# Five and four seven-product pairs in a feed-forward pass, raw low parts on GpSimd

## The chip, the core and the metric

One core of a Trainium2 chip runs the whole kernel. The metric is device time in microseconds from one launch, median of three runs. Its engines run side by side, each with its own instruction queue, and are kept in order by semaphores: TensorE multiplies, VectorE and ScalarE and GpSimd do elementwise work, SyncE issues the loads. TensorE, VectorE and ScalarE read and write the accumulator banks, and all of them share the on-chip memory SBUF.

## What is computed

One layer of a hybrid decoder on 256 tokens with a model width of 2048: a latent attention and a state-space branch, merged and projected, then a SwiGLU feed-forward part, then a gated per-layer embedding. The change lies in the feed-forward part:

```
f = rms_norm(h, ffn_norm_pre)                       # 256 x 2048
f = (silu(f @ w_gate) * (f @ w_up)) @ w_down        # w_gate, w_up: 2048 x 5632
h = h + rms_norm(f, ffn_norm_post)
```

All is float32, and the result has to be close to float32.

## The kernel before

**Precision.** A float32 value is held as a high part (`whi`, rounded to TensorE's fp32r) and a low part (`wlo = raw - whi`, fp32r too). One product of a 128x128 block of tokens with 512 weight columns is three matmuls: high by high, high by low, low by high (`one_tile`; matmuls L851 to L853).

**Passes and chunks.** The feed-forward phase `ff` has 11 passes (0 to 10). A pass covers 512 columns of `w_gate` and the same 512 of `w_up`, side by side as one 1024-column row block, and runs over the 2048 rows as 16 chunks of 128 rows. SyncE loads a chunk by two DMAs of 256 KB into one of four slots of `raw` (`load`, L534). ScalarE makes the high part (`split`, L1351), VectorE the low part (`split`, L1914), TensorE does four block products (2 halves of the columns by 2 blocks of tokens), 12 matmuls. A slot of `raw` is loaded again once the semaphore `lo_ready` says that its low part is done; `whi` and `wlo` have the same four slots and are free when `chunk_done` says that TensorE is through.

**Pairs.** Two chunks make a pair. As 2x2 blocks (two row blocks by gate and up columns; two token blocks) a pair is eight block products. A pair in `SEVEN` is done by seven products of sums and differences (Strassen-Winograd), 21 matmuls (L912 to L914), against 24. For that VectorE forms three sums of weight blocks (`seven_sums`, L1973, L1980, L1982: t0 and t1 in one instruction, then t2, t3) in `tr_ff`, ScalarE makes their high parts `thi_ff` (`seven_high`, L1381), VectorE their low parts `tlo_ff` (L1991), which lie in the same bytes as the sums. The left half of a seven pair's first chunk needs no low part (so ScalarE and VectorE treat 1024 and 512 columns: L1374, L1375, L1977, L1984). The differences of the token blocks (`xf_new`) are made once, during pass 0 (`operand_sums` L1943 to L1950, `operand_high` L1361, `operand_low` L1957), and serve all passes. Passes 1 to 9 have three seven pairs, pass 10 two. Their order within a pass is the list `PAIRS["ff"]` = (3, 4, 0, 5, 1, 6, 2, 7): each seven pair (0, 1, 2) stands between plain ones.

**End of a pass.** The seven-product results collect in extra banks and are merged: ScalarE copies one (L1391), VectorE forms three combinations (L2011, L2013, L2015) and, in the next pass, folds them into the accumulators (L2057, L2055). Then ScalarE applies Silu (`ff_gate`, L1788), VectorE multiplies gate by up (`ff_product`, L2758), TensorE transposes (L1242), ScalarE and VectorE make the high (L1795) and low part (`ff_low`, L2765) of the down-projection's input. In passes 1 to 4 also operands for the down-projection are made, at chunks 11 (sums), 12 (high), 14 (low).

**Order.** Each engine's program is written out by hand in order; nothing is reordered. GpSimd does no arithmetic on tensors: it only issues DMAs, among them the parking of `h` in DRAM (L611) before pass 1, and the next one after pass 10.

Of the kernel before, what the change touches and what calls it, by code (L numbers as in the profile page):

```python
# [50 lines left out]
P = 128  # L51
# [25 lines left out]
FF_THREES = (1, 2, 3, 4, 5, 6, 7, 8, 9)  # L77
PASSES = (("so", 0), ("so", 1), ("ao", 0), ("ao", 1), ("wo", 0)) + tuple(("ff", _j) for _j in range(1, FF_LAST + 1)) \
# [5 lines left out]
SEVEN.update({("ff", _j): (0, 1, 2) if _j in FF_THREES else (0, 1) for _j in range(1, FF_LAST + 1)})  # L84
# [8 lines left out]
}  # L93
PAIRS_AT = {"so": 16, "ao": 16, "wo": 0, "ff": 0, "dn": 0, "pg": 0}
MERGE = {_p: PAIRS_AT[_p[0]] + 2 * PAIRS[_p[0]].index(SEVEN[_p][-1]) + 2 for _p in PASSES}
SEVENS_BEFORE = {_p: sum(len(SEVEN[_q]) for _q in PASSES[:_i]) for _i, _p in enumerate(PASSES)}
OPERANDS = (("so", 0, 3), ("so", 3, 2), ("so", 5, 2), ("ao", 0, 3), ("wo", 0, 3), ("ff", 0, 1), ("ff", 1, 1), ("ff", 2, 1),
            ("dn", 0, 2), ("dn", 2, 2), ("dn", 4, 2), ("dn", 6, 2), ("dn", 8, 1), ("pg", 0, 2))
AO_OPERANDS, WO_OPERANDS, FF_OPERANDS, DN_OPERANDS, PG_OPERANDS = 3, 4, 5, 8, 13
# [48 lines left out]
def build(nc, x, p_in, positions, mix_norm_pre, mix_norm_post, w_in, q_norm, w_uq, kv_norm, w_ukv,  # L148
# [52 lines left out]
    def at(name, shape, offset, dt=F32):  # L201
# [78 lines left out]
                      at("xf_new2", [P, 1, 2, 4, P], G0 + 36 * 2048, F32R)]}  # L280
# [8 lines left out]
    for ph, t_at, hi_at in (("so", H0 + 8192, G0 + 32 * 2048), ("ao", H0, H0 + 8192),  # L289
# [5 lines left out]
        s_u[ph] = at("s_u_" + ph, [P, 2, 512], hi_at)  # L295
    raw_f, whi_f, wlo_f = (w[:, :, :].rearrange("p r n -> p (r n)") for w in (raw, whi, wlo))
# [90 lines left out]

    TURNS = ("ff",)
# [119 lines left out]
    def _(sp):  # L508
# [21 lines left out]
        for phase, (per, its) in PHASES.items():  # L530
# [3 lines left out]
            def load(it, c):  # L534
# [12 lines left out]
            if its == 1 or phase in TURNS or phase == "ssm":  # L547
                for c_ in range(per):
                    load(0, c_)
                first = 1  # L550
            if its > 1:
# [13 lines left out]
    def _(pool):  # L565
        pool.wait_ge(sem("x_in11"), 16)
        for v, dst in ((dt_bias, dtb), (a_log, alog), (d_skip, dsk)):
            pool.dma_start(dst[:, :], v.partition_broadcast(P)).then_inc(sem("heads_in"), 16)

        pool.wait_ge(sem("cumt_ev"), 1)  # L570
        pool.dma_start(cum_dram, cumt[:, :]).then_inc(sem("cum_out"), 16)
        pool.wait_ge(sem("cum_out"), 16)
# [38 lines left out]
        pool.dma_start(h_dram, h[:, :, :]).then_inc(sem("h_park"), 16)  # L611
        pool.wait_ge(sem("chunk_done"), num("dn", 0, 8))
# [17 lines left out]
    def _(pe):  # L630
# [255 lines left out]
        def seven_products(phase, it, c):  # L886

            begin(phase, it, c + 1)
            p = pair_of(phase, it, c)
            n = SEVEN[phase, it].index(p)  # L890
            src, t0 = (u, 0) if phase in FROM_U else (g, WO_TILE if phase == "wo" else 0)
# [25 lines left out]
            product(c_bank(phase, it, 1, 0), tokens(t0 + 2 * p + 1, 0), weights(slot + 1, 1))  # L917
# [7 lines left out]
            product(v_bank(phase, it, 3), differences(3) if phase in KEPT else tokens(2 * p, 1), sums(1), first, last)  # L925
# [53 lines left out]
        def rotary_key():  # L979
# [5 lines left out]
            T.matmul(bank(4)[:, SEQ:2 * SEQ], dupk, kr[0:64, :], start=True, stop=True).then_inc(sem("krot_mm"), 1)  # L985
# [5 lines left out]
            last.then_inc(sem("rt_mm"), 1)  # L991

        pe.wait_ge(sem("raw_sum"), GROUPS * 3 + 3)
        for it in range(2):
# [72 lines left out]
        def attn_main(it, c_):  # L1067
# [86 lines left out]
        for it in range(2):  # L1154
# [185 lines left out]
    def _(act):  # L1340
# [12 lines left out]
        def operand_high(k):  # L1353
# [3 lines left out]
            if (ph, first) == ("so", 3):  # L1357
                act.wait_ge(sem("c_park"), 16)
# [7 lines left out]
        def seven_high(phase, it, c, between=None):  # L1366
# [32 lines left out]
        def rstd(src, tmp, name, n, scale=1.0):  # L1399
# [3 lines left out]
            S.activation(tmp, src, ACT.Ln, scale=scale).then_inc(sem("rstd_ln"), 1)  # L1403
            act.wait_ge(sem("rstd_ln"), lns[0])
# [112 lines left out]
        for c_ in range(20):  # L1517
# [52 lines left out]
        def so_gate(it):  # L1570
# [89 lines left out]
        def ao_gate(it):  # L1660
# [5 lines left out]
            last.then_inc(sem("sg_ao"), 1)  # L1666
# [109 lines left out]
        def ff_gate(j):  # L1776
# [22 lines left out]

# [1152 lines left out]
```

## Time and profile before

| | us |
|---|---|
| median of three runs | 1993.66 |
| lowest, highest | 1993.58, 1994.48 |
| span of the profiled execution | 1992.0 |
| TensorE busy | 1979.0 (99%) |
| VectorE busy | 1668.8 (84%) |
| ScalarE busy | 1147.6 (58%) |
| GpSimd busy | 18.9 (1%) |

The profile records one execution. A line of a view names the engine, the source line, the operation, the tiles written and read and their shapes. PE is TensorE, PEld its weight loads, DVE VectorE, ACT ScalarE, POOL GpSimd, SPq SyncE's queue. A matmul's listed time overlaps that of its neighbours, so its cost in a stream is read from start to start.

### The profile page before, as it was taken

The numbers are of one execution on the slowest core, as the hardware profiler recorded it, in microseconds if no ns is written. First come the engines' busy times: TensorE is split into PE (matmuls) and PEld (weight loads), VectorE is DVE, ScalarE is ACT, GpSimd is POOL, SyncE is SP. The second block draws the span as 40 slices with busy tenths as digits, with TensorE's granted clock in tenths as the row PEclk, the third lists the DMA queues.
The fourth block names the chain that finished last, engine by engine and source line by source line (L and its number), as shares of the span: only waits on it lengthen the run. The fifth ranks groups of instructions, "written<-read, shape, count | busy, mean of one in ns | idle before, by whom it ended". The sixth has DMA issues, their size and how long they took to land.

```text
span 1992.0 us, 29428 instructions
## 1 busy us (share of the span) xinstructions
PE 1979.0 (99%) x10149; PEld 1681.0 (84%) x10149; DVE 1668.8 (84%) x2336; ACT 1147.6 (58%) x1482; POOL 18.9 (1%) x37
## 2 busy tenths in 40 slices
PE   9999999999999999999999999999999999999998
PEld 8888888888888888998888888888888888888886
DVE  7788888889888868767777787999999988888887
ACT  6666566666655545565545565556555555555575
POOL 0000000000000000000000000000000000000000
PEclk9999999999999999999999999999999999999999
DMA  8666676666566566545556667666566666766754
GB/s 235 200 191 190 190 206 184 188 192 195 172 207 209 189 203 223 156 132 156 191 191 239 205 207 242 189 202 202 190 201 200 200 201 201 254 201 207 244 189 152
DMA packets 255197, 394.74 MB, mean 198 GB/s; under 512 B 28840, under 2 KB 161440, under 8 KB 252928
## 3 DMA queue, kind: packets, MB, share of 16 engines
q1 hardware_dynamic: 251104, 369.87, 59.7%
q0 software_dynamic: 3824, 23.43, 3.5%
q8 instruction: 58, 0.95, 0.2%
q14 instruction: 35, 0.29, 0.0%
q10 hardware_dynamic: 176, 0.20, 0.0%
HBM read 387.08 MB, written 6.36 MB: 198 GB/s over the span
## 4 chain that ended last, share of the span: by engine, by line
PE 98%; DVE 1%; ACT 0%; DMA 0%; issue 0%; DVEq 0%; SPq 0%; ACTq 0%
PE acc L655 16%; PE acc L851 15%; PE acc L853 15%; PE acc L852 15%; PE acc L660 8%; PE acc L912 6%; PE acc L913 6%; PE acc L914 6%; PE acc L1107 1%; PE acc L785 1%; PE acc L637 1%; PE acc L636 1%; PE acc L638 1%; PE acc L1038 1%; PE acc L1242 0%; PE acc L714 0%
## 5 line engine op out<-in xcount | busy, mean ns | idle before, releaser
L1914 DVE TENSOR_TENSOR wlo<-raw,whi 128x1024 fp32r<-128x1024 f32 (+2 forms) x559 | 662.5, 1205 | 110.8 <-ACT whi L1351 108.3
L1351 ACT ACTIVATE whi<-raw 128x1024 fp32r<-128x1024 f32 (+1 forms) x560 | 572.2, 1044 | 244.4 <-PE acc L853 81.7
L655 PE MATMUL acc<-u,whi 128*128 128x512 f32 x1376 | 328.7, 391 | 0.0
L851 PE MATMUL acc<-whi,u 128*128 128x512 f32 x824 | 323.0, 392 | 0.1
L853 PE MATMUL acc<-whi,u 128*128 128x512 f32 x824 | 320.8, 389 | 0.0
L852 PE MATMUL acc<-wlo,u 128*128 128x512 f32 x824 | 320.6, 389 | 0.0
L655 PEld LDWEIGHTS acc<-u,whi 128*128 128x128 f32 x1376 | 252.7, 188 | 48.8
L851 PE MATMUL acc<-whi,g 128*128 128x512 f32 x520 | 202.8, 390 | 0.1
L853 PE MATMUL acc<-whi,g 128*128 128x512 f32 x520 | 202.4, 389 | 0.0
L852 PE MATMUL acc<-wlo,g 128*128 128x512 f32 x520 | 202.3, 389 | 0.0
L1374 ACT ACTIVATE whi<-raw 128x1024 fp32r<-128x1024 f32 x72 | 76.5, 1062 | 209.9 <-PE acc L914 162.0
L660 PEld LDWEIGHTS acc<-u,wlo 128*128 128x128 f32 x1376 | 178.1, 191 | 8.3 <-issue 1.5
L660 PE MATMUL acc<-u,wlo 128*128 128x256 f32 x1376 | 184.6, 284 | 0.0
L851 PEld LDWEIGHTS acc<-whi,u 128*128 128x128 f32 x824 | 154.7, 188 | 32.8 <-ACT park L1771 0.6
L853 PEld LDWEIGHTS acc<-whi,u 128*128 128x128 f32 x824 | 154.7, 188 | 32.3
L852 PEld LDWEIGHTS acc<-wlo,u 128*128 128x128 f32 x824 | 154.8, 188 | 31.2
L851 PEld LDWEIGHTS acc<-whi,g 128*128 128x128 f32 x520 | 97.7, 188 | 20.9 <-DVE wlo L1914 0.5
L853 PEld LDWEIGHTS acc<-whi,g 128*128 128x128 f32 x520 | 97.6, 188 | 20.3
L852 PEld LDWEIGHTS acc<-wlo,g 128*128 128x128 f32 x520 | 97.6, 188 | 20.0
L1977 DVE TENSOR_TENSOR wlo<-raw,whi 128x1024 fp32r<-128x1024 f32 x72 | 87.6, 1217 | 0.1
L1381 ACT ACTIVATE thi_ff<-tr_ff 128x1024 fp32r<-128x1024 f32 x58 | 60.0, 1053 | 23.6 <-DVE tr_ff L1982 23.6
L1991 DVE TENSOR_TENSOR tlo_ff<-tr_ff,thi_ff 128x1024 fp32r<-128x1024 f32 x58 | 68.2, 1216 | 0.0
(597 smaller groups left out, 2990.8 us busy)
## 6 DMA issues: line engine op xcount, KB each, us to landing
raw<-w_in_in SPq DMA_DIRECT2D x208, 512.0 KB, 3.8
raw<-w_gate_in SPq DMA_DIRECT2D x176, 256.0 KB, 3.0
raw<-w_up_in SPq DMA_DIRECT2D x176, 256.0 KB, 3.3
raw<-w_down_in SPq DMA_DIRECT2D x88, 512.0 KB, 4.6
raw<-w_ssm_o_in SPq DMA_DIRECT2D x64, 512.0 KB, 4.3
raw<-w_in_in SPq DMA_DIRECT2D x64, 256.0 KB, 4.0
raw<-w_attn_o_in SPq DMA_DIRECT2D x32, 512.0 KB, 4.7
raw<-w_out_in SPq DMA_DIRECT2D x32, 512.0 KB, 4.9
```

Source lines behind the costliest of these rows:

```text
L655: return T.matmul(bank(banks[i]), wh[:, j, i * P:i * P + P], src[:, kts[j], :, :].rearrange("p a s -> p (a s)"), start=start and j == 0, s ...
L660: return T.matmul(bank(banks[i])[:, 0:SEQ], wl[:, j, i * P:i * P + P], src[:, kts[j], 0, :], start=False, stop=not lows_first and stop and ...
L851: T.matmul(o, x_hi, wh[:, j, :], start=start, stop=False, skip_group_check=True)
L852: T.matmul(o, x_hi, wl[:, j, :], start=False, stop=False, skip_group_check=True)
L853: return T.matmul(o, x_lo, wh[:, j, :], start=False, stop=stop, skip_group_check=True)
L912: T.matmul(bank(b), xs[0], ws[0], start=start, stop=False, skip_group_check=True)
L913: T.matmul(bank(b), xs[0], ws[1], start=False, stop=False, skip_group_check=True)
L914: return T.matmul(bank(b), xs[1], ws[0], start=False, stop=stop, skip_group_check=True)
L1351: S.activation(whi[:, slot, 0:w], raw[:, slot, 0:w], ACT.Copy).then_inc(sem("hi_ready"), 1)
L1374: S.activation(whi_f[:, inner], raw_f[:, inner], ACT.Copy).then_inc(sem("hi_ready"), 1)
L1914: V.tensor_tensor(wlo[:, slot, 0:w], raw[:, slot, 0:w], whi[:, slot, 0:w].bitcast(F32), ALU.subtract) \
L1977: V.tensor_tensor(wlo_f[:, inner], raw_f[:, inner], whi_f[:, inner].bitcast(F32), ALU.subtract) \
```

## The change

Raw weights' low parts of passes 1 to 9 are computed by GpSimd. Passes 1 to 7 have five seven-product pairs, adjacent to each other, pass 8 four, pass 9 three as before. In passes 1 to 8 the sums are kept in `ts_ff`, apart from their low parts. TensorE takes the first product of a seven pair after a first piece (`first_lo`), and the second chunk's right half after the fourth product. VectorE makes a pair's first sum before the low parts of the second half of the pair before. Two more token operands are made in pass 0. The down-projection operands' high and low parts move to chunk 1 of the next pass. The loads of `ff` are written out rather than looped. Several semaphores elsewhere are merged under new names (for space in their number), with the same order of work; this part is left out below.

```diff
+FF_FOURS = (8,)
+FF_FIVES = (1, 2, 3, 4, 5, 6, 7)
+FF_APART = FF_FOURS + FF_FIVES
+POOLED = tuple(("ff", _j) for _j in FF_THREES)
-SEVEN.update({("ff", _j): (0, 1, 2) if _j in FF_THREES else (0, 1) for _j in range(1, FF_LAST + 1)})
+SEVEN.update({("ff", _j): tuple(range(5 if _j in FF_FIVES else 4 if _j in FF_FOURS else 3 if _j in FF_THREES else 2))
+              for _j in range(1, FF_LAST + 1)})
+PAIRS.update({("ff", _j): (5, 6, 0, 1, 2, 3, 4, 7) for _j in FF_FIVES})
+PAIRS.update({("ff", _j): (4, 5, 0, 1, 6, 2, 3, 7) for _j in FF_FOURS})
...
+    ts_ff = at("ts_ff", [P, 4, 512], G0 + 32 * 2048)
...
@@ SyncE, load()
                 sp.wait_ge(sem("lo_ready"), num(phase, it, c) - RING + 1)
+                if phase == "ff" and isinstance(it, int):
+                    it_, c_ = (it, c - RING) if c >= RING else (it - 1, c - RING + PHASES["ff"][0])
+                    if is_pooled("ff", it_) and is_seven("ff", it_, c_):
+                        n = SEVENS_BEFORE["ff", it_] + SEVEN["ff", it_].index(pair_of("ff", it_, c_))
+                        sp.wait_ge(sem("t_sum"), 3 * n + (3 if c_ % 2 else 1))
@@ GpSimd, after the parking of h
+        def raw_low(it, c):
+            slot = c % RING
+            pool.wait_ge(sem("hi_ready"), num("ff", it, c) + 1)
+            G.tensor_tensor(wlo[:, slot, :], raw[:, slot, :], whi[:, slot, :].bitcast(F32), ALU.subtract) \
+                .then_inc(sem("lo_ready"), 1)
+        def seven_raw_low(it, c):
+            slot = c % RING
+            pool.wait_ge(sem("hi_ready"), num("ff", it, c) + 1)
+            G.tensor_tensor(wlo[:, slot, 512:], raw[:, slot, 512:], whi[:, slot, 512:].bitcast(F32), ALU.subtract) \
+                .then_inc(sem("first_lo"), 1)
+            G.tensor_tensor(wlo[:, slot + 1, 0:512], raw[:, slot + 1, 0:512], whi[:, slot + 1, 0:512].bitcast(F32),
+                            ALU.subtract).then_inc(sem("lo_ready"), 1)
+            pool.wait_ge(sem("hi_ready"), num("ff", it, c + 1) + 1)
+            G.tensor_tensor(wlo[:, slot + 1, 512:], raw[:, slot + 1, 512:], whi[:, slot + 1, 512:].bitcast(F32),
+                            ALU.subtract).then_inc(sem("lo_ready"), 1)
@@ TensorE, seven_products()
-            begin(phase, it, c + 1)
+            if pooled:
+                pe.wait_ge(sem("first_lo"), pooled_before(it, n) + 1)
+            else:
+                begin(phase, it, c + 1)
             product(v_bank(phase, it, 0), tokens(t0 + 2 * p, 0), weights(slot, 1), first, last)
-            product(c_bank(phase, it, 1, 0), tokens(t0 + 2 * p + 1, 0), weights(slot + 1, 1))
+            if pooled:
+                begin(phase, it, c)
+            else:
+                product(c_bank(phase, it, 1, 0), tokens(t0 + 2 * p + 1, 0), weights(slot + 1, 1))
...
+            if pooled:
+                begin(phase, it, c + 1)
+                product(c_bank(phase, it, 1, 0), tokens(t0 + 2 * p + 1, 0), weights(slot + 1, 1))
             pe.wait_ge(sem("t_lo"), 2 * done + 2)
@@ ScalarE, seven_high()
+                if is_pooled(phase, it) and half == 0:
+                    act.wait_ge(sem("t_used"), n)
+                if is_pooled(phase, it) and half and is_seven(phase, it, c - 1):
+                    act.wait_ge(sem("chunk_done"), num(phase, it, c))
                 act.wait_ge(sem("t_sum"), 3 * n + 1 + 2 * half)
@@ VectorE
+        def pooled_sums(phase, it, c, between=None):
+            ...
+            behind, ahead = is_seven(phase, it, c - 1), is_seven(phase, it, c + 2)
+            for i in range(2):
+                dve.wait_ge(raw_in[slot + i], loads(phase, it, c + i) * 16)
+            dve.wait_ge(sem("chunk_done"), num(phase, it, c + 1) - RING + 1)
+            if behind:
+                dve.wait_ge(sem("t_lo"), 2 * n - 1)
+            V.tensor_tensor(t[:, 0:2, :], ..., ALU.add).then_inc(sem("t_sum"), 1)
+            if behind:
+                sums_low(phase, it, n - 1, 1)
+                dve.wait_ge(sem("t_lo"), 2 * n)
+            dve.wait_ge(sem("t_sum"), 3 * n + 1)
+            V.tensor_tensor(t[:, 2, :], t[:, 0, :], raw[:, slot + 1, 0:512], ALU.add).then_inc(sem("t_sum"), 1)
+            dve.wait_ge(sem("t_sum"), 3 * n + 2)
+            V.tensor_tensor(t[:, 3, :], t[:, 2, :], raw[:, slot + 1, 512:], ALU.add).then_inc(sem("t_sum"), 1)
+            if between:
+                between()
+            sums_low(phase, it, n, 0)
+            if not ahead:
+                sums_low(phase, it, n, 1)
```

## Rows read from the trace of the kernel before

**Rows 1.** The page: busy time by engine, and the chain that ended last.
```profile
PE 1979.0 (99%) x10149; PEld 1681.0 (84%) x10149; DVE 1668.8 (84%) x2336; ACT 1147.6 (58%) x1482; POOL 18.9 (1%) x37
...
PE 98%; DVE 1%; ACT 0%; DMA 0%; issue 0%; DVEq 0%; SPq 0%; ACTq 0%
```

**Rows 2.** Stretches: us; busy PE, PEld, DVE, ACT, POOL; clock; DMA share; GB/s.
```profile
1190.00:1232.00 42.00, 42.00 (x195) 34.97 (x194) 33.20 (x57) 25.44 (x43) 0.53 (x1) 1.00 0.79 271
...
1316.80:1359.20 42.40, 42.40 (x193) 35.18 (x192) 41.06 (x46) 25.10 (x29) 0.00 (x0) 1.00 0.63 199
...
1401.60:1444.00 42.40, 42.40 (x193) 35.20 (x192) 38.36 (x40) 23.15 (x26) 0.00 (x0) 1.00 0.62 199
```

**Rows 3.** Order of time, TensorE, pass 3: start, duration, instruction.
```profile
1333.23 0.39 PE L851 MATMUL acc<-whi,u 128*128 128x512 f32 x1
...
1338.67 0.39 PE L912 MATMUL acc<-whi,u 128*128 128x512 f32 x1
...
1343.43 0.39 PE L851 MATMUL acc<-whi,u 128*128 128x512 f32 x1
```

**Rows 4.** Order of time, VectorE: a seven pair and the plain pair behind it.
```profile
1333.55 1.22 DVE L1973 TENSOR_TENSOR tr_ff<-raw 128x1024 f32<-128x1024 f32 x1
1334.68 1.22 DVE L1977 TENSOR_TENSOR wlo<-raw,whi 128x1024 fp32r<-128x1024 f32 x1
1335.82 0.68 DVE L1980 TENSOR_TENSOR tr_ff<-tr_ff,raw 128x512 f32<-128x512 f32 x1
1336.54 0.69 DVE L1982 TENSOR_TENSOR tr_ff<-tr_ff,raw 128x512 f32<-128x512 f32 x1
1337.15 0.68 DVE L1984 TENSOR_TENSOR wlo<-raw,whi 128x512 fp32r<-128x512 f32 x1
1337.75 2.35 DVE L1991 TENSOR_TENSOR tlo_ff<-tr_ff,thi_ff 128x1024 fp32r<-128x1024 f32 x2
1340.02 2.35 DVE L1914 TENSOR_TENSOR wlo<-raw,whi 128x1024 fp32r<-128x1024 f32 x2
```

**Rows 5.** Order of time, VectorE: gated product, its low part, a pass's end.
```profile
1320.57 1.40 DVE L2758 SCALAR_TENSOR_TENSOR fu<-acc,st,sgate 128x512 f32<-128x512 f32 x2
...
1327.87 1.23 DVE L2765 TENSOR_TENSOR g<-acc,g 128x1024 fp32r<-128x1024 f32 x1 [0.56 <-ACT xd_full L1797]
...
1355.91 1.22 DVE L2015 TENSOR_TENSOR s_u_ff<-tr_ff,acc 128x1024 f32<-128x1024 f32 x1
...
1359.32 1.23 DVE L2057 TENSOR_TENSOR acc<-acc,s_u_ff 128x1024 f32<-128x1024 f32 x1
```

**Rows 6.** GpSimd: groups (busy, mean ns), and its last DMA ahead of pass 1.
```profile
L600 POOL DMA_DIRECT2D h<-x_in x4 | 2.2, 540 | 56.7 <-PE acc L853 56.7
...
L2921 POOL MEMSET const-bfloat16-1.0<- 128x1 bf16 x1 | 0.1, 95 | 0.0
...
1203.89 0.53 POOL L611 DMA_DIRECT2D h_scratch<-h  x1 [15.08 <-ACT junk_w L1731]
```

**Rows 7.** Order of time, ScalarE, a seven pair of pass 3.
```profile
1333.51 1.06 ACT L1374 ACTIVATE whi<-raw 128x1024 fp32r<-128x1024 f32 x1 [1.89 <-PE acc L914]
...
1335.00 1.04 ACT L1381 ACTIVATE thi_ff<-tr_ff 128x1024 fp32r<-128x1024 f32 x1
```

**Rows 8.** The page's DMA issues: count, KB each, median us to landing.
```profile
raw<-w_gate_in SPq DMA_DIRECT2D x176, 256.0 KB, 3.0
raw<-w_up_in SPq DMA_DIRECT2D x176, 256.0 KB, 3.3
```

**Rows 9.** Order of time, pass 0: an operand on VectorE; the normalisation's reader on ScalarE.
```profile
1208.26 0.75 DVE L1943 TENSOR_TENSOR xf_full<-u 128x256 f32<-128x256 f32 x2
...
1210.11 1.22 DVE L1914 TENSOR_TENSOR wlo<-raw,whi 128x1024 fp32r<-128x1024 f32 x1
...
1232.04 1.27 ACT L1788 ACTIVATE sgate<-acc,st 128x512 f32<-128x512 f32 x2 [0.30 <-PE acc L853]
```

**Rows 10.** VectorE's low parts of the whole run: shortest, median, longest in ns.
```profile
L1914 DVE TENSOR_TENSOR wlo<-raw,whi x559: 683/1217/1227, 19.0 to 1973.8; 128x1024 fp32r<-128x1024 f32 x179, 128x768 fp32r<-128x768 f32 x6, 128x512 fp32r<-128x512 f32 x2
```

More of the change, by code:

```diff
@@ L140, in is_seven, with is_pooled, pooled_before @@
     return (phase, it) in PASSES and pair_of(phase, it, c) in SEVEN[phase, it]
+def is_pooled(phase, it):
+    return isinstance(it, int) and (phase, it) in POOLED
+def pooled_before(it, n):
+    return sum(len(SEVEN["ff", _j]) for _j in FF_THREES if _j < it) + n
 def num(phase, it, c):
@@ L385, in build @@
     D_IN = w_in.shape[1]
-    TURNS = ("ff",)
     RD_AT, X_AT = (1, 3, 4, 6), (0, 2, 5, 7)
@@ L550, in _ @@
                 first = 1
-            if its > 1:
+            if phase == "ff":
+                for it_ in range(its):
+                    for c_ in range(per):
+                        load(it_, c_)
+            elif its > 1:
                 with sp.Fori(first, its) as it:
@@ L611, in _ @@
         pool.dma_start(h_dram, h[:, :, :]).then_inc(sem("h_park"), 16)
+        G = nc.gpsimd
+        def raw_low(it, c):
[13 more added lines that the diff above has]
+                            ALU.subtract).then_inc(sem("lo_ready"), 1)
+        pool.wait_ge(sem("lo_ready"), num("ff", FF_THREES[0], 0))
+        for it in FF_THREES:
+            for c_ in range(16):
+                if not is_seven("ff", it, c_):
+                    raw_low(it, c_)
+                elif c_ % 2 == 0:
+                    seven_raw_low(it, c_)
         pool.wait_ge(sem("chunk_done"), num("dn", 0, 8))
@@ L924, in seven_products @@
                 pe.wait_ge(sem("ff_lo"), FF_LAST + 1)
-            product(v_bank(phase, it, 3), differences(3) if phase in KEPT else tokens(2 * p, 1), sums(1), first, last)
+            product(v_bank(phase, it, 3), differences(3) if phase in KEPT else tokens(2 * p, 1), sums(1), first, last) \
+                .then_inc(sem("t_used"), 1)
+            if pooled:
+                begin(phase, it, c + 1)
+                product(c_bank(phase, it, 1, 0), tokens(t0 + 2 * p + 1, 0), weights(slot + 1, 1))
             pe.wait_ge(sem("t_lo"), 2 * done + 2)
@@ L2155, in tables @@
                     link(last)
-            last.then_inc(sem("gp_all"), 1)
-            dve.wait_ge(sem("gp_all"), 1)
+            link(last)
         def prepare_dt():
@@ L2564, in ao_evac @@
             group_end("ao", it, 31)
-            dve.wait_ge(sem("sg_ao"), it + 1)
+            dve.wait_ge(sem("sigmoid"), it + 3)
             folded("ao", it, half)
             gated, cols = sg[:, :, 512 * half:512 * half + 512], slice(512 * n, 512 * n + 512)
-            V.tensor_tensor(gated, psum[:, 4 + 2 * half:6 + 2 * half, :], gated, ALU.mult).then_inc(sem("ao_ev"), 1)
-            dve.wait_ge(sem("ao_ev"), n + 1)
+            link(V.tensor_tensor(gated, psum[:, 4 + 2 * half:6 + 2 * half, :], gated, ALU.mult))
             V.tensor_tensor(m[:, :, cols], gated, m[:, :, cols], ALU.add).then_inc(sem("mixed"), 1)
@@ L2734, in _ @@
         u_low(0, 3, V_FFPRE)
-        for c_ in range(6, 8):
-            split("ff", 0, c_)
+        split("ff", 0, 6)
+        operand_sums(FF_OPERANDS)
+        split("ff", 0, 7)
         hidden_norm(1, "h_r")
```

126 lines of the change are left out of this document (78 added, 48 removed).

## The prediction

> **What bounds the kernel now.** I read the page's busy shares and the chain that ended last first [rows 1]: TensorE is busy for 99% of the span and is 98% of the chain, VectorE 84%, ScalarE 58%, GpSimd 1%. So only fewer matmuls, or a wait put in front of them, can move the time. Then I read the stretches pass by pass [rows 2]: a feed-forward pass takes 42.40 us, TensorE fills all of it at a granted clock of 1.00 (its 2.4 GHz level), VectorE is busy 41.06 us in a pass that also prepares a down-projection operand (pass 3) and 38.36 us in one that doesn't (pass 5), ScalarE 23 to 25 us. VectorE is therefore the next bound and nearly reached, which is why more seven-product pairs can't be had without taking work off it. TensorE waits for nothing in these passes: the 42.40 us are full.
>
> The price of a pair is in TensorE's order of time [rows 3]. A pair done by seven products runs from 1338.67 to 1343.43, 4.76 us for 21 matmuls; a plain pair (two chunks) from 1333.23 to 1338.67, 5.44 us for 24. One matmul thus costs 0.227 us in the stream (its listed 0.39 us overlaps its neighbours), and a pair changed from plain to seven saves 0.68 us.
>
> **The change, part by part.**
>
> *Matmuls removed.* Passes 1 to 7 get two more seven-product pairs each, pass 8 one: 15 pairs x 0.68 = 10.2 us off the bounding engine. Passes 1 to 7 become 42.40 - 1.36 = 41.04 us, pass 8 41.72, pass 9 stays. Nothing else on TensorE changes in number; the product of the second tile's right half moves behind the fourth product.
>
> *Work moved off VectorE.* A plain pair costs it two splits, 2.27 us from start to start (as the two instructions from 1337.75 to 1340.02), a seven pair 6.47 us (1333.55 to 1340.02) [rows 4]. Of that the raw weights' low parts are 1.14 and 0.60; what stays is 1.13 + 0.72 + 0.61 for the three sums and 2.27 for the sums' low parts, 4.73 us (I read costs from start to start, since listed durations overlap). Per pass: 5 x 4.73 = 23.7, plus the closing sums and folds (two of 0.7, three of 1.2: 5.0 [rows 4, 5]), the gated product and its low part (1.4 + 1.2 [rows 5]), in all 31 us and some 3 more with an operand. VectorE has room over a pass. Within a run of adjacent seven pairs it has none: the first sum of a pair now waits for the first low part of the pair before, an end-to-start wait like the 0.11 us that separates a dependent pitch (0.72) from a free one (0.61) [rows 4], so a pair takes about 4.85 us against TensorE's 4.76. Over five pairs it falls back by 0.4 us; the slack below covers that.
>
> *Work put on GpSimd.* Per seven pair three subtractions of 512 columns, per plain pair two of 1024. The trace shows no GpSimd arithmetic on weights. Lower bound: VectorE's same instruction, 1.22 and 0.68 us [rows 4]. Upper bound: its two operands read one after the other, twice VectorE's time, plus the 0.54 us of a GpSimd queue instruction [rows 6]: 2.98 and 1.90 us. I take the doubled time without the 0.54, 2.43 and 1.37, because GpSimd's own small memsets show only 0.09 us an instruction [rows 6]. Then a seven pair takes it 4.1 us of 4.76, a plain pair 4.9 of 5.44, a pass 5 x 4.11 + 6 x 2.43 = 35.1 of 41.0: it keeps up. The Trainium skill (GPSIMD Engine Reference, Performance versus the Vector engine) gives 4497 ns for a 2048-column fp32 tensor_tensor; by that an estimate is 2.25 and 1.12 us and a pass 30.4, also within the time. No row here shows it.
>
> *The latencies.* Take as time 0 the moment at which TensorE ends pair k-2 and begins k-1, and use ScalarE's times [rows 7]. ScalarE first does the second half of the sums' high part of k-1 (it waits for pair k-2) to 1.1, then the raw high part of k to 2.1, then 0.5 more. GpSimd's three pieces end at 3.6, 4.9 and 6.3; TensorE asks for them at 4.76, 5.44 and 7.5. VectorE: first sum to 1.2, low part of k-1's second half to 2.4 (TensorE asks at 3.4), two sums to 3.8, low part of k's first half to 5.0 (asked at 6.1). All are in time by 0.5 to 1.2 us. The weakest link is the ring: the second slot is given back at 6.3 instead of early in the pair, its two transfers, issued one behind the other, land 3.0 and 3.3 us after issue [rows 8], which makes it about 10.1; the first sum of k+2 (wanted at 9.6) then ends at 11.2 and the low part behind it at 12.4, TensorE asks at 12.9. A landing half a microsecond late stalls TensorE. The bandwidth is there: 1 MB per 4.76 us is 220 GB/s, and pass 0 ran at 271 GB/s [rows 2]. After the last seven pair chunk 14 needs a whole 1024-column low part: ready at 4.6, asked at 4.76. For these I allow 0.4 us in each of the seven passes, 2.8 us; bounds 0 and 1.36 (what the pass saved).
>
> *Small parts, at no cost.* Two more operands in pass 0: 1.85 us of sums each on VectorE [rows 9] and a 512-column low part, 0.7, so 5.1 us in a stretch where it is busy 33.2 of 42.0 [rows 2]; without that room TensorE would wait for its low parts; the normalisation behind the first comes 1.9 us later, and its reader, Silu of pass 0, comes 22 us after those sums [rows 9]. Down-projection operands move from chunks 11 to 14 into the next pass's chunk 1, first used after all passes. ScalarE gets 5 x 3.5 us of seven pairs for 3 x 3.5 and loses four splits of 1.0, +3 us on 25. The feed-forward loads are written out instead of looped; nothing TensorE sees, as long as the loads land in time. Renamed semaphores change no order. GpSimd's DMAs stand behind its new work, but the next is due in the down-projection; the one ahead, the parking of h, is issued at 1203.9 [rows 6], 28 us before pass 1.
>
> **Sum.** -10.2 + 2.8 = -7.4 us. The profiled execution's span is 1992.0 us, so 1984.6; the median of the runs is 1.7 us above that span, so 1993.7 - 7.4 = 1986.3. Own range: 1983.3 (no stall, 1983.5, less the runs' spread) to 1989.6.
>
> **Rivals.**
>
> *A. VectorE and GpSimd take turns at SBUF (slower).* All of what VectorE keeps in a seven pair has both inputs in SBUF, as has every new GpSimd instruction. If such instructions exclude one another, their times add: 5 x 4.73 + 35.1 = 58.8 us a pass against 41.0, so TensorE waits for low parts. That is +16.4 us over 42.4 in seven passes, +12.4 in pass 8 (35.9 + 18.9), +8.4 in pass 9 (36.6 + 14.2) and some 10 us for the operands in four passes: +146, 2139 us. With half of the time overlapped, about 2060; with GpSimd as fast as VectorE (17.6 + 23.7 = 41.3) there would be no loss against 42.4. It decides as soon as the two together pass 42.4 us a pass. For it: both must read two fp32 streams out of one memory at once, which no stretch of this trace does. Against it: no row shows VectorE slowed by anything, its subtraction of weights has a median of 1.217 us and a longest of 1.227 [rows 10], but GpSimd is idle there, so that is weak. The Trainium skill (SBUF — State Buffer, Who interferes with whom) states just this: a VectorE instruction with two SBUF inputs contends with a GpSimd one that reads SBUF, and the later one blocks until the first is finished. It speaks against the change; with the page's GpSimd time of above the same sum would be an estimate of 2097 us. No run here shows it yet.
>
> *B. GpSimd is too slow by itself (slower).* From 1.59 us per 512 columns on (4.76 / 3) it bounds the seven pairs. At the upper bound a seven pair is 5.70, a plain 5.96, a pass 46.4: +4.0 x 7 + 4.2 + 4.5 = +37, 2030 us.
>
> *C. The saving is eaten (no change).* The ring gives the slots back so late that each of the 35 side-by-side pairs waits 0.3 us for its weights: 10 us back, 1993 to 1995. For it: the ring is the link with the least slack in the sum above. Against it: a landing has 0.5 us to spare at the median.
>
> *D. The matmuls don't fall as said.* The new table of pairs is plain to read; if it held only in part, the same result as C.
>
> **Chances.** Forecast (faster) 0.47; A 0.28, of which 0.10 above 2110; B 0.12; C and D 0.13. The likeliest time is 1986.3. The range has to reach into A: from 1983 (0.04 lie below) to 2110 leaves some 0.14 out. A measurement of this kernel tells about 0.2% (4 us) from no change. Faster by more 0.47, within 0.13, slower 0.40.
>
> **What would show it.** Right: TensorE's passes 1 to 7 at 41.0 to 41.4 us with 177 wide matmuls in place of 183, VectorE's busy time down to 31 to 34 us a pass, GpSimd at 30 to 36, VectorE's 1024-column subtraction still 1.22 us. A: subtractions of VectorE and of GpSimd stretched, or never side by side in the order of time, TensorE waiting for the low parts of weights and sums. B: GpSimd busy without a gap at over 1.59 us per 512 columns. C: waits of ScalarE and VectorE on raw transfers, TensorE behind them. The forecast falls if any of these outgrows 1.4 us a pass.

## The result, and the profile after

The changed kernel takes 2115.1 us (2115.0 to 2115.3, four runs) against 1993.6 us before: a ratio of 1.061, interval 1.059 to 1.062. It is 121.5 us slower, where 7.4 us faster was forecast. The profiled execution spans 2113.6 us.

The page of the changed kernel, busy time and the chain that ended last, beside [rows 1]:

```profile
PE 2000.5 (95%) x10104; PEld 1670.6 (79%) x10104; DVE 1750.2 (83%) x2281; ACT 1174.1 (56%) x1514; POOL 397.8 (19%) x223
...
PE 20%; DVE 8%; issue 1%; DMA 0%; ACT 0%; DVEq 0%; SPq 0%; ACTq 0%
...
L658 POOL TENSOR_TENSOR wlo<-raw,whi 128x1024 fp32r<-128x1024 f32 x60 | 148.2, 2495 | 71.0 <-ACT whi L1430 71.0
...
L2151 DVE TENSOR_TENSOR tlo_ff<-ts_ff,thi_ff 128x1024 fp32r<-128x1024 f32 x78 | 128.7, 1651 | 0.4
```

TensorE executes 45 matmuls fewer, as meant (15 pairs by 3). Its busy time nevertheless rises by 21.5 us: listed times overlap in an unbroken stream, while the matmul before a wait counts with its whole 0.39 us and the one behind it is listed with 0.50. VectorE was to lose a large part of its work and yet is busy for 81 us more: it has 55 instructions fewer, and those it keeps last longer. Its low part of the sums, listed at 1.22 us throughout before (two in 2.35, [rows 4]), has a mean of 1651 ns. The printed chain explains only some 30% of the span; it is no use here, and I read the stretches and the waits instead.

Stretches of the changed kernel for passes 1, 4, 6 and 9 (us; busy PE, PEld, DVE, ACT, POOL; clock; DMA share; GB/s), beside [rows 2], and then TensorE's longest waits in the whole run (total, times, longest):

```profile
1232.40:1289.70 57.30, 46.22 (x195) 35.04 (x196) 48.74 (x34) 26.89 (x31) 45.65 (x22) 1.00 0.50 157
...
1410.00:1467.90 57.90, 44.06 (x180) 32.99 (x179) 53.37 (x38) 27.30 (x32) 42.22 (x21) 0.97 0.44 141
1525.10:1579.70 54.60, 43.66 (x187) 33.36 (x186) 46.48 (x33) 26.54 (x30) 41.64 (x22) 1.00 0.49 154
1685.80:1733.80 48.00, 43.64 (x192) 34.77 (x191) 38.85 (x25) 23.37 (x26) 38.27 (x18) 1.00 0.56 175
```

```profile
PE acc L984 <- DVE tlo_ff L2151: 91.0, 67, 2.3
PE acc L919 <- POOL wlo L658: 7.6, 4, 1.9
```

About 120 of the 121.5 us lie in passes 1 to 9. From the feed-forward transposes of one pass to those of the next (they stand behind chunk 2 of every pass) I read these distances in TensorE's order of time, in us, for all kernels of this study (the names are those of the experiments below):

```
pass                 1     2     3     4     5     6     7     8     9    10
before             42.4  42.4  42.4  42.4  42.3  42.4  42.4  42.4  42.4  43.1
after              57.4  59.3  60.9  58.0  57.2  54.6  54.6  51.5  48.1  43.1
pool8              43.2  43.2  43.3  43.2  42.3  42.3  42.3  41.9  42.4  43.1
memset             43.1  43.1  43.1  43.1  42.1  42.1  42.1  41.9  42.4  43.1
copy               46.9  46.9  46.9  47.0  46.0  46.0  46.0  43.1  42.4  43.1
pool8_sums8        43.2  42.1  42.1  42.1  41.2  41.2  41.2  41.9  42.4  43.1
threes_pool        50.8  53.0  52.6  52.5  50.7  48.4  48.2  48.2  48.1  43.1
fives_dve          51.4  52.0  52.0  52.0  50.5  49.2  49.2  44.9  42.4  43.1
sums8              58.6  56.2  53.5  55.7  51.0  50.4  50.4  47.5  48.4  43.1
control            43.9  44.5  44.5  44.5  42.9  42.4  42.4  42.4  42.4  43.1
control_old        42.4  42.4  42.4  42.4  42.4  42.4  42.4  42.4  42.4  43.1
pool8_old          44.6  44.6  44.6  44.6  42.3  42.3  42.3  41.9  42.4  43.1
```

The order of time shows what happens in a pair. VectorE in the run of seven pairs of pass 3, changed kernel, one whole period, beside [rows 4]:

```profile
1380.97 1.23 DVE L2166 TENSOR_TENSOR ts_ff<-raw 128x1024 f32<-128x1024 f32 x1
1382.11 2.32 DVE L2151 TENSOR_TENSOR tlo_ff<-ts_ff,thi_ff 128x1024 fp32r<-128x1024 f32 x1
1384.46 1.66 DVE L2173 TENSOR_TENSOR ts_ff<-ts_ff,raw 128x512 f32<-128x512 f32 x1
1386.16 1.67 DVE L2175 TENSOR_TENSOR ts_ff<-ts_ff,raw 128x512 f32<-128x512 f32 x1
1387.75 1.21 DVE L2151 TENSOR_TENSOR tlo_ff<-ts_ff,thi_ff 128x1024 fp32r<-128x1024 f32 x1
1389.09 1.23 DVE L2166 TENSOR_TENSOR ts_ff<-raw 128x1024 f32<-128x1024 f32 x1
```

GpSimd in the same stretch:

```profile
1381.88 1.47 POOL L665 TENSOR_TENSOR wlo<-raw,whi 128x512 fp32r<-128x512 f32 x1 [2.73 <-ACT whi L1453]
1383.31 2.26 POOL L667 TENSOR_TENSOR wlo<-raw,whi 128x512 fp32r<-128x512 f32 x1
1385.54 1.74 POOL L670 TENSOR_TENSOR wlo<-raw,whi 128x512 fp32r<-128x512 f32 x1
...
1390.01 1.47 POOL L665 TENSOR_TENSOR wlo<-raw,whi 128x512 fp32r<-128x512 f32 x1 [2.73 <-ACT whi L1453]
```

A period is 8.12 us, where TensorE needs 4.76. GpSimd has three instructions in it, and exactly three of VectorE's five are lengthened: 2.32, 1.66 and 1.67 us for 1.22, 0.7 and 0.7, by about 1 us each. The two that start while GpSimd is idle have their old length. GpSimd's own three take 1.47, 2.26 and 1.74 us here; what they take alone is measured below. GpSimd's last starts at 1385.54 and ends at 1387.28; VectorE's next begins its count at 1386.16 and ends at 1387.83, that is, it runs only once GpSimd is done. GpSimd isn't the bound by its own length: before each first piece it is idle for 2.73 us. TensorE meanwhile, same kernel:

```profile
1387.11 0.39 PE L986 MATMUL acc<-whi,xf_new 128*128 128x512 f32 x1
1389.01 0.51 PE L984 MATMUL acc<-thi_ff,xf_new 128*128 128x512 f32 x1 [1.52 <-DVE tlo_ff L2151]
```

It waits for the low part of the sums (L2151), 67 times in the trace, 91 us. So the engines of a run wait in a circle: VectorE's chain sets the low parts, TensorE ends the pair, only then ScalarE's high part of the next may start, and behind that GpSimd.

### The profile page after: what moved, and what is told of

Same layout as the page of the kernel before. It is cut to its first block and busy times, and to the rows that moved or that the text cites. A ratio compares the mean times of both kernels' runs of the same rounds, so it can differ in the third digit from the quotient of the medians.

```text
span 2113.6 us, 29052 instructions
## 1 busy us (share of the span) xinstructions
PE 2000.5 (95%) x10104; PEld 1670.6 (79%) x10104; DVE 1750.2 (83%) x2281; ACT 1174.1 (56%) x1514; POOL 397.8 (19%) x223
## 5 line engine op out<-in xcount | busy, mean ns | idle before, releaser
L1430 ACT ACTIVATE whi<-raw 128x1024 fp32r<-128x1024 f32 (+1 forms) x530 | 542.2, 1043 | 244.0 <-PE acc L921 73.9
L2000 DVE TENSOR_TENSOR wlo<-raw,whi 128x1024 fp32r<-128x1024 f32 (+1 forms) x469 | 556.4, 1205 | 107.7 <-ACT whi L1430 105.6
L919 PE MATMUL acc<-whi,u 128*128 128x512 f32 x704 | 278.5, 396 | 7.8 <-POOL wlo L658 7.6
L921 PE MATMUL acc<-whi,u 128*128 128x512 f32 x704 | 275.2, 391 | 0.0
L920 PE MATMUL acc<-wlo,u 128*128 128x512 f32 x704 | 275.0, 391 | 0.0
L1464 ACT ACTIVATE thi_ff<-ts_ff 128x1024 fp32r<-128x1024 f32 x78 | 81.9, 1057 | 151.8 <-DVE ts_ff L2175 125.6
L919 PEld LDWEIGHTS acc<-whi,u 128*128 128x128 f32 x704 | 132.7, 188 | 40.1 <-POOL wlo L658 11.3
L658 POOL TENSOR_TENSOR wlo<-raw,whi 128x1024 fp32r<-128x1024 f32 x60 | 148.2, 2495 | 71.0 <-ACT whi L1430 71.0
L921 PEld LDWEIGHTS acc<-whi,u 128*128 128x128 f32 x704 | 132.5, 188 | 28.0
L920 PEld LDWEIGHTS acc<-wlo,u 128*128 128x128 f32 x704 | 132.7, 189 | 26.3
L984 PE MATMUL acc<-thi_ff,xf_new 128*128 128x512 f32 x132 | 59.4, 450 | 91.0 <-DVE tlo_ff L2151 91.0
L2151 DVE TENSOR_TENSOR tlo_ff<-ts_ff,thi_ff 128x1024 fp32r<-128x1024 f32 x78 | 128.7, 1651 | 0.4
L919 PEld LDWEIGHTS acc<-whi,g 128*128 128x128 f32 x520 | 97.6, 188 | 22.0 <-DVE wlo L2000 1.1
```

The source lines that it names most:

```text
L658: G.tensor_tensor(wlo[:, slot, :], raw[:, slot, :], whi[:, slot, :].bitcast(F32), ALU.subtract) \
L919: T.matmul(o, x_hi, wh[:, j, :], start=start, stop=False, skip_group_check=True)
L920: T.matmul(o, x_hi, wl[:, j, :], start=False, stop=False, skip_group_check=True)
L921: return T.matmul(o, x_lo, wh[:, j, :], start=False, stop=stop, skip_group_check=True)
L984: T.matmul(bank(b), xs[0], ws[0], start=start, stop=False, skip_group_check=True)
L1430: S.activation(whi[:, slot, 0:w], raw[:, slot, 0:w], ACT.Copy).then_inc(sem("hi_ready"), 1)
```

## The experiments

My theory after the result was rival A (VectorE instructions with both inputs in SBUF and GpSimd instructions that read SBUF take turns). Against it stood B (GpSimd is slow by itself) and the side-by-side order with its waits and its ring (C, in a stronger form).

**The disputed cost by itself.** A kernel of twelve stages: VectorE, GpSimd and ScalarE each run a row of independent instructions beside one another, with a meeting of all three between stages.

```diff
+def tt(E, o, i0, i1, n, k):
+    for j in range(k):
+        last = E.tensor_tensor(o[:, j * n:j * n + n], i0[:, 0:n], i1[:, 0:n], ALU.subtract)
+    return last
...
+        g.meet(tt(V, vo["big"], a, b, 1024, 16))      # VectorE, both inputs in SBUF
+        g.meet(tt(V, vo["ps"], ps, b, 1024, 16))      # VectorE, first input in the banks
...
+        g.meet(tt(G, go["big"], c, d, 1024, 8))       # GpSimd, beside the first
+        g.meet(tt(G, go["ps"], c, d, 1024, 8))        # GpSimd, beside the second
...
```

> Twelve stages with a meeting of VectorE, GpSimd and ScalarE between them; nothing of the layer is computed, the output is a copy of x. Theory A (VectorE instructions with both inputs in SBUF and GpSimd instructions that read SBUF take turns): GpSimd alone takes about 1.1 us per 512 columns and 2.3 per 1024, VectorE alone 0.6 and 1.14. Together, the shorter list's instructions come out in between: per pair of one 512-column instruction of each about 1.7 us, of 1024 columns about 3.4 us. With VectorE's first input in the accumulator banks, or with ScalarE beside it, GpSimd stays at 2.3 us and VectorE at 1.14. GpSimd memsets beside VectorE: no effect on either. GpSimd copies with one input beside VectorE: turns again, about 0.6 us plus the copy. Rival (the two share a port by cycles, without turns): both are stretched by a similar factor, and no instruction of 256 columns waits for as long as a GpSimd instruction of 1024. Rival B (GpSimd is slow by itself): 512 columns over 1.59 us alone.

The groups of this kernel (busy us, mean ns); VectorE's `v_x` and GpSimd's `g_x` of one name run side by side, `alone` has only one engine at work:

```profile
L71 DVE TENSOR_TENSOR v_big<-a,b 128x1024 fp32r<-128x1024 f32 x16 | 35.4, 2284 | 0.0
L71 DVE TENSOR_TENSOR v_tt<-a,b 128x512 fp32r<-128x512 f32 x24 | 31.6, 1391 | 16.1 <-POOL g_alone L71 16.1
L71 POOL TENSOR_TENSOR g_big<-c,d 128x1024 fp32r<-128x1024 f32 x8 | 26.3, 3318 | 5.5 <-issue 5.5
L71 POOL TENSOR_TENSOR g_tt<-c,d 128x512 fp32r<-128x512 f32 x16 | 26.3, 1678 | 0.1
L71 DVE TENSOR_TENSOR v_cp<-a,b 128x512 fp32r<-128x512 f32 x24 | 21.1, 955 | 0.0
L71 POOL TENSOR_TENSOR g_ps<-c,d 128x1024 fp32r<-128x1024 f32 x8 | 18.5, 2356 | 9.2 <-issue 9.2
...
L71 POOL TENSOR_TENSOR g_act<-c,d 128x1024 fp32r<-128x1024 f32 x8 | 18.5, 2337 | 0.1
L71 POOL TENSOR_TENSOR g_alone<-c,d 128x1024 fp32r<-128x1024 f32 x8 | 18.4, 2340 | 0.1
...
L71 DVE TENSOR_TENSOR v_ps<-ps,b 128x1024 fp32r<-128x1024 f32 x16 | 18.2, 1211 | 0.0
...
L109 POOL COPY g_cp<-c 128x512 f32<-128x512 f32 x16 | 16.3, 1068 | 6.7 <-issue 6.7
L71 DVE TENSOR_TENSOR v_ms<-a,b 128x1024 fp32r<-128x1024 f32 x12 | 13.7, 1218 | 16.2 <-POOL g_act L71 16.2
L71 POOL TENSOR_TENSOR g_alone<-c,d 128x512 fp32r<-128x512 f32 x8 | 9.8, 1262 | 9.1 <-DVE v_alone L71 9.1
...
L71 DVE TENSOR_TENSOR v_alone<-a,b 128x1024 fp32r<-128x1024 f32 x8 | 9.2, 1217 | 0.0
```

Divide busy time by count. Alone, GpSimd takes 18.4 / 8 = 2.30 us per 1024 columns and 9.8 / 8 = 1.23 per 512, VectorE 9.2 / 8 = 1.15 per 1024. Side by side with 1024 columns, GpSimd takes 26.3 / 8 = 3.29, close to the 3.45 of both in turn; VectorE's 16 take 35.4, which is 8 turns of 3.29 and 8 alone at 1.14. With 512 columns a turn is 26.3 / 16 = 1.64 against 1.23 + 0.60 = 1.83. So the turns are nearly pure, with 0.16 to 0.19 us of each hidden. With VectorE's first input in the banks (`ps`) neither engine is slower, with ScalarE beside it (`act`) GpSimd isn't, and beside GpSimd memsets (`ms`) VectorE isn't (13.7 / 12 = 1.14 us). A GpSimd copy (`cp`, one input) takes turns again: 16.3 / 16 = 1.02 us a turn, and VectorE's 24 take 21.1 us, 16 turns and 8 alone at 0.60. The rule of turns holds as expected. In a further stage 24 VectorE instructions of 256 columns ran beside four GpSimd instructions of 1024:

```profile
L71 DVE TENSOR_TENSOR v_small<-a,b x24: 408/410/2608, 209.7 to 226.1; 128x256 fp32r<-128x256 f32 x24
```

The shortest and the median are 0.41 us, the longest 2.61: a short one waits for a whole GpSimd instruction, and four of the 24 do. That speaks against sharing by cycles. A turn costs at least what the GpSimd instruction in it lasts, however small VectorE's is.

**GpSimd's work cut to 8 columns.**

```diff
-            G.tensor_tensor(wlo[:, slot, :], raw[:, slot, :], whi[:, slot, :].bitcast(F32), ALU.subtract) \
+            G.tensor_tensor(wlo[:, slot, 0:8], raw[:, slot, 0:8], whi[:, slot, 0:8].bitcast(F32), ALU.subtract) \
...
```

> The changed kernel with every GpSimd subtraction cut to 8 columns; the rest of the raw weights' low parts in passes 1 to 9 is left out. All waits, orders, pairs and buffers stay. Theory A: what costs is the SBUF time of GpSimd's instructions, so the forecast's account comes back: 1983 to 1987 us. Rival (the waits, the ring or the side-by-side order of seven pairs cost the time): stays above 2050 us.

Measured 1997.2 us, ratio 1.0016 (1.0006 to 1.0026). So 118 of the 121.5 us go with the length of GpSimd's subtractions, and waits, ring and side-by-side order are not the rival they were made. This run by itself doesn't tell turns from slowness of GpSimd; the kernel of stages and the runs below do. The expected 1983 to 1987 is missed as well: the run stays 10.9 us above the forecast's 1986.3 even when GpSimd's work is next to nothing. VectorE in the run of pass 2 of this kernel:

```profile
1299.66 1.23 DVE L2164 TENSOR_TENSOR ts_ff<-raw 128x1024 f32<-128x1024 f32 x1
1300.80 1.23 DVE L2149 TENSOR_TENSOR tlo_ff<-ts_ff,thi_ff 128x1024 fp32r<-128x1024 f32 x1
1302.06 0.73 DVE L2171 TENSOR_TENSOR ts_ff<-ts_ff,raw 128x512 f32<-128x512 f32 x1
1302.83 0.69 DVE L2173 TENSOR_TENSOR ts_ff<-ts_ff,raw 128x512 f32<-128x512 f32 x1
1303.43 1.22 DVE L2149 TENSOR_TENSOR tlo_ff<-ts_ff,thi_ff 128x1024 fp32r<-128x1024 f32 x1
1304.79 1.23 DVE L2164 TENSOR_TENSOR ts_ff<-raw 128x1024 f32<-128x1024 f32 x1
```

VectorE never pauses, and the period is 1304.79 - 1299.66 = 5.13 us against TensorE's 4.76. From start to start the steps are 1.14, 1.26, 0.77, 0.60, 1.36; three of them end in a wait for the result before. The 8.12 us of the changed kernel are these 5.13 and three delays of 1.0. TensorE shows the 0.37 us as short delays, most of them too short to be listed as waits: where a pair first needs the second half's low parts, two matmuls start 0.45 us apart instead of 0.23.

**Memsets and copies in place of subtractions.**

```diff
-            G.tensor_tensor(wlo[:, slot, :], raw[:, slot, :], whi[:, slot, :].bitcast(F32), ALU.subtract) \
+            G.memset(wlo[:, slot, :].bitcast(F32), 0.0) \        # memset
+            G.tensor_copy(wlo[:, slot, :], raw[:, slot, :]) \    # copy
```

> The changed kernel with GpSimd's subtractions replaced by memsets of the same columns (write only, nothing read); low parts of raw weights in passes 1 to 9 are left out. Theory A with a lock on reading alone: 1983 to 1990 us. If writes take turns too: each piece still costs VectorE its memset's time, 2010 us or more.

> The changed kernel with GpSimd's subtractions replaced by copies of the same columns of raw (one input from SBUF); the subtraction of the high part is left out. Theory A: a copy of 512 columns takes perhaps 0.5 us, so a seven pair takes 4.73 + 3 x 0.5 = 6.2 us against 4.76, five of them 7 us too long: some 5 us a pass over the kernel before, 2025 to 2045 us. If only two-input instructions of GpSimd contend: 1983 to 1990 us.

Memsets: 1995.7 us (ratio 1.0009, 0.9999 to 1.0019), so writing alone takes no turns; it lies above the expected 1990, for the reason just seen with 8 columns. VectorE's period in a run is 5.09 us here, so 0.04 of the 5.13 were still turns with the 8-column subtractions and the rest is VectorE's own. Copies: 2024.0 us, 1 us under what was expected: 27 us over the run with 8 columns, from GpSimd instructions that read one input.

**Only the move to GpSimd, only the pairs.**

```diff
-FF_FOURS = (8,)
-FF_FIVES = (1, 2, 3, 4, 5, 6, 7)
+FF_FOURS = ()                      # threes_pool
+FF_FIVES = ()
```

```diff
 def pooled_sums(...):              # fives_dve; GpSimd's part taken out, plain chunks by VectorE's split()
             V.tensor_tensor(t[:, 0:2, :], ..., ALU.add).then_inc(sem("t_sum"), 1)
+            dve.wait_ge(sem("hi_ready"), num(phase, it, c) + 1)
+            V.tensor_tensor(wlo_f[:, inner], raw_f[:, inner], whi_f[:, inner].bitcast(F32), ALU.subtract) \
+                .then_inc(sem("lo_ready"), 1)
...
```

> Only the move to GpSimd: three seven pairs in passes 1 to 9 in the old order, raw low parts by GpSimd. Theory A: each pass has 9 x 1.2 + 10 x 2.3 us of GpSimd and 3 x 4.7 of VectorE's two-input work, 48 us, as pass 9 of the changed kernel shows (48.05); 5.7 us x 9 and some 8 us for the operands make 2053 us. Rival (the loss comes from five pairs side by side): within 5 us of the kernel before.

> The changed kernel with all pairs, orders and buffers, but the raw low parts made by VectorE between its own sums instead of by GpSimd. By the side-by-side period of 5.13 us that the run with 8-column GpSimd work shows, a seven pair takes VectorE 5.13 + 1.14 + 0.60 = 6.9 us, five of them 10.6 us more than TensorE's 4.76, so a pass some 48 us: about 2040 us in all. Theory A then says that moving the low parts to GpSimd made the kernel slower than leaving the same pairs on VectorE would (2115). Rival: VectorE's overload is worse than taking turns, over 2115.

The move alone takes 2065.3 us (expected 2053), the five pairs alone 2056.2 (expected 2040), both together 2115. So either half loses, and five pairs are better off on an overloaded VectorE than with GpSimd's help: with VectorE making the raw low parts too, its period in a run is 6.82 us (pass 6, 1502.70 to 1509.52) against the 8.12 of the changed kernel, and none of its subtractions is lengthened. In passes 6 to 9 the move alone takes 48.1 to 48.4 us; the sum of turns is 9 x 1.23 + 10 x 2.30 + 3 x 4.73 = 48.3. That the sum is met this closely is in part chance: GpSimd is idle for 6.4 of the 48 us, and the turns hide some time in one another. Passes 2 to 4 are 4.3 us longer, where I had put some 2 us a pass for the operands; what makes up the rest is not shown.

**VectorE's part cut.** Two runs cut its third and fourth sums to 8 columns in passes 2 to 8, one with GpSimd's work at 8 columns, one with all of it.

```diff
+            w = 8 if it in range(2, 9) else 512
-            V.tensor_tensor(t[:, 2, :], t[:, 0, :], raw[:, slot + 1, 0:512], ALU.add).then_inc(sem("t_sum"), 1)
+            V.tensor_tensor(t[:, 2, 0:w], t[:, 0, 0:w], raw[:, slot + 1, 0:w], ALU.add).then_inc(sem("t_sum"), 1)
...
```

> GpSimd's subtractions cut to 8 columns as before, and in passes 2 to 8 also VectorE's third and fourth sums cut to 8 columns; raw low parts and two sums are left out. If what is left of the loss without turns (1997 instead of 1986) is VectorE's chain of 5.13 us a side-by-side pair, it falls by 1.0 to 4.1, below TensorE's 4.76, and the passes go to 41.1 us (2 to 4 perhaps 0.9 more for the wait on ScalarE's copy): 1986 to 1990 us. If it is the ring of loads or the waits of TensorE on pieces: no change, 1997.

> The changed kernel with GpSimd's full work, and VectorE's third and fourth sums cut to 8 columns in passes 2 to 8 (two sums left out). Theory A: times add, so the 1.04 us that VectorE saves per seven pair come off its turn-taking sum: 5.2 us in each of passes 2 to 7 and 4.2 in pass 8, 2080 us. Rival B (GpSimd's own length bounds the passes): no change, 2115.

With both cut: 1990.7 us, ratio 0.9984 (0.9975 to 0.9993), 0.7 us above the expected range. Passes 5 to 7 come to 41.2 us, which is the 41.04 of the forecast, and passes 2 to 4 stay 0.9 above. So the residue of the 8-column run in passes 5 to 7 is VectorE's chain. With GpSimd at full work: 2084.5 us, expected 2080. Passes 6 and 7 fall by 4.2 us each for 5.2 saved by the sum; passes 2 to 5 fall unevenly, by 2.3 to 7.4. Rival B, by which VectorE's length wouldn't matter, is out here too.

**The small parts.**

```diff
-FF_FIVES = (1, 2, 3, 4, 5, 6, 7)     # control: as threes_pool, and
-POOLED = tuple(("ff", _j) for _j in FF_THREES)
+POOLED = ()
...
-                if it <= 4 and c_ == 15:      # control_old, pool8_old: operand steps at their old chunks
+                if it <= 4 and c_ == 11:
                     operand_sums(DN_OPERANDS + it - 1)
+                if it <= 4 and c_ == 14:
+                    operand_low(DN_OPERANDS + it - 1)
...
```

> Everything of the change except its two main parts: three seven pairs in passes 1 to 9 in the old order, raw low parts by VectorE, GpSimd without arithmetic; the written-out loads, the two more operands of pass 0, the moved down-projection operands and the merged semaphores stay. Forecast's 'small parts at no cost': 1993.6 within 2 us. Rival (the small parts cost something): 1996 us or more.

> As control, and the down-projection operands' steps put back to chunks 11 (sums), 12 (high) and 14 (low) of their own pass. If moving them cost the 8.7 us (passes 1 to 5 of control take 43.9, 44.5, 44.5, 44.5 and 42.9 us for 42.4): 1993.6 to 1995 us, all passes at 42.4. Rival (the fifth and fourth operand of pass 0, the loads or the semaphores cost it): stays at 2000 or more.

> GpSimd's subtractions cut to 8 columns (raw low parts of passes 1 to 9 left out) and the down-projection operands' steps at their old places. In that run passes 1 to 4 take 43.2 us for 42.3 in 5 to 7. If the moved steps cost this too: passes 1 to 4 at 42.3, 1993 to 1994 us. Rival (VectorE waits 2.5 us for ScalarE's extra copy of the gated product in these passes, and the pair behind has no slack to make it up): no change, 1997.

The control takes 2002.6 us, ratio 1.0043 (1.0029 to 1.0056), not the expected 1993.6; the kernel before took 1993.95 beside it. So the small parts cost 8.7 us when VectorE has the low parts. With the operand steps back at chunks 11 to 14 it is 1994.4 (1.0003, 0.9994 to 1.0012). Hence the move of these steps is the whole of it within about 1 us, and the pass-0 operands, the written-out loads and the semaphores are free to that measure. The reason stands in VectorE's and TensorE's order of time of the control, end of pass 3:

```profile
1360.71 1.22 DVE L2100 TENSOR_TENSOR s_u_ff<-tr_ff,acc 128x1024 f32<-128x1024 f32 x1
1361.85 0.42 DVE L2032 TENSOR_TENSOR xd_sum<-xd_full 128x256 f32<-128x256 f32 x1
...
1363.44 2.35 DVE L1999 TENSOR_TENSOR wlo<-raw,whi 128x1024 fp32r<-128x1024 f32 x2
```

```profile
1364.81 0.47 PE L918 MATMUL acc<-whi,u 128*128 128x512 f32 x1 [0.77 <-DVE wlo L1999]
```

The 1.6 us of operand sums now stand behind the closing sums and ahead of the raw low part that TensorE needs next. Over the whole run TensorE has eight listed waits for VectorE's raw low parts, 3.9 us, where the kernel before has none; the rest of the 8.7 isn't split up here. In the 8-column run the old places are worse, 2002.4 us against 1997.2, and passes 1 to 4 go from 43.2 to 44.6: there chunk 11 lies inside the run of seven pairs. So the expected 1993 was wrong, and the 0.9 us by which passes 1 to 4 exceed 5 to 7 isn't cured by moving. In the twice-cut kernel VectorE stands idle in front of its gated low part, for 3.55 us in a pass in which ScalarE makes an extra copy first (pass 3), and for 2.93 in one in which it doesn't (pass 6):

```profile
1329.87 1.23 DVE L2887 TENSOR_TENSOR g<-acc,g 128x1024 fp32r<-128x1024 f32 x1 [3.55 <-ACT xd_full L1880]
1331.01 1.22 DVE L2149 TENSOR_TENSOR tlo_ff<-ts_ff,thi_ff 128x1024 fp32r<-128x1024 f32 x1
...
1454.33 1.22 DVE L2887 TENSOR_TENSOR g<-acc,g 128x1024 fp32r<-128x1024 f32 x1 [2.93 <-ACT g L1878]
```

So the wait is there in both, and the copy (1.0 us, made in passes 1 to 4 only) lengthens it by 0.6 us. That fits as a part of the 0.9 us, but it is only argued; no run took the copy out.

## Why the prediction was wrong

- **Matmuls removed: right.** 45 fewer matmuls; with all else out of the way passes 5 to 7 take 41.2 us for the 41.04 forecast.
- **Work put on GpSimd: the step that failed.** The price of an instruction was sized well: 1.23 and 2.30 us for 1.37 and 2.43, well inside the bounds. What failed was to let it run beside VectorE's chain at no cost to either. I compared GpSimd's 35.1 us with the pass and VectorE's 31 us with the pass, each by itself, and gave the rule that forbids it 0.28. Their two-input work adds up: 15 x 1.23 + 6 x 2.30 + 23.7 = 56.0 us, measured 54.6 in passes 6 and 7. The Trainium skill (SBUF — State Buffer, Who interferes with whom) was right against the forecast; here its rule shows with 3.29 us for a pair of 1024-column instructions in turn. Its other figure (GPSIMD Engine Reference, Performance versus the Vector engine), 4497 ns per 2048 columns, agrees with 2.30 us per 1024, and the estimate of 2097 us from the two was 18 us off, where rival A's own 2139 us was 24 off.
- **VectorE within a run: mis-sized.** I took 4.85 us a pair and let the slack cover it. It is 5.13 (5.09 beside memsets), because there are three dependent steps, not two, and the one into the next pair costs 1.36. Over five pairs that is 1.85 us behind TensorE's 4.76 each, more than the slack covers: passes 5 to 7 come out 1.3 us long instead of the 0.4 allowed.
- **Latencies: wrong link.** I held the ring and the landing of loads for the weakest. In the passes of the 8-column run TensorE's listed waits are for the low parts of the sums, and in none of the runs' longest waits of TensorE stands a transfer. Rival C's mechanism is not seen. That its time (no change) is nearly what the 8-column run gives is chance: there it is VectorE's chain.
- **Small parts at no cost: wrong in one.** I looked only at when the down-projection operands are first used, not at what stands behind their steps on VectorE. With the low parts on VectorE the move costs 8.2 us (2002.6 against 1994.4).
- **Rival A: right in mechanism.** It was given for 2060 to 2139 us. In the changed kernel it costs 118 us over the 8-column run, a small part of which may be the clock. In passes 3 to 5 the mean granted clock is 0.97: from 1369.8 to 1373.2, behind waits of 1.86 and 2.09 us, it is 0.50 (1.2 GHz), and matmuls start 0.43 us apart instead of 0.23. There are four such stretches in these passes and pass 8, some 2 us each, so 8 us at most. The run with only the move shows that they cost less than that: its passes 6, 7 and 8 have one each and take 48.4, 48.2 and 48.2 us, and pass 9 has none and takes 48.1.
- **Rival B: out.** Alone GpSimd takes 1.23 us for 512 columns, under the 1.59 that B needs, and it is idle for 2.73 us in every pair of a run.
- **The range** held its end at 2110 and missed 2115 by 5 us: I cut rival A's span by a chance, although the arithmetic of turns left little room under 2097.

No version that beats the kernel before came out of this. Even with raw low parts nearly free (8 columns, or memsets) the five pairs side by side gave 1995.7 to 1997.2 us, because VectorE's own chain is then the bound. The 1990.7 us of the twice-cut kernel leave out two sums a pair besides.

## What to carry to other kernels

Before moving fp32 elementwise work from VectorE to GpSimd, add, for each stretch between two pieces that TensorE waits for, GpSimd's time and the time of VectorE's instructions with two SBUF inputs; if the sum exceeds the stretch, the move loses, and each instruction moved adds twice what it takes off (2.30 us for 1.14). In these runs GpSimd's subtractions were free beside VectorE instructions with one input in an accumulator bank and beside ScalarE, and its memsets cost VectorE nothing. A short VectorE copy from SBUF to SBUF did wait, as shown below. For a chain that repeats back to back, add the dependent start-to-start distances and compare them with the bounding engine's period: slack hides a single delay, never one that comes again in every turn.

## What the runs showed of the hardware that was not expected

- Whether GpSimd takes turns with VectorE depends on its reading SBUF, not on the number of its inputs: copies (one input) gave 1.02 us a turn of 512 columns, memsets none.
- Turns are dealt singly: sixteen VectorE subtractions of 1024 columns beside eight of GpSimd took eight turns of 3.29 us and eight of 1.14. Neither engine got two in a row while the other had one ready.
- A VectorE copy of 8 columns from SBUF to SBUF, one input only, also waited for a whole GpSimd instruction: 2370 ns, for the 171 that it takes when GpSimd has nothing running, while a 1024-column copy out of the banks kept its 1.21 us. In the groups of the kernel of stages, first the long copy from the banks, then the short one beside GpSimd and alone:

```profile
L89 DVE COPY v_copy<-ps 128x1024 f32<-128x1024 f32 x16 | 18.2, 1212 | 0.0
...
L85 DVE COPY v_tiny<-a 128x8 f32<-128x8 f32 x1 | 2.4, 2370 | 0.5 <-DVE v_ps L71 0.5
...
L80 DVE COPY v_tiny<-a 128x8 f32<-128x8 f32 x1 | 0.2, 171 | 0.0
```
